# Fetching the first tile's experts beside the last mLSTM cells, with private buffers for its mixer

## The reference

```python
h = modulate(rmsnorm(x, n1), sh1, sc1)
mq, mk, mv, mo, gt, aq, ak, av = split_cols(h @ w_in)
m_out = mlstm_mixer(...)          # both directions, chunk by chunk: a recurrence over C, n, m
a_out = attn_latent(...)          # windowed attention with sinks, 8 heads
x = x + g1 * (concat([m_out, a_out]) @ w_out)
h2 = modulate(rmsnorm(x, n2), sh2, sc2)
q = h2 @ w_q                      # 8 heads x 2 halves of 128
va, ia = top_k(q_a . sub_a, 16); vb, ib = top_k(q_b . sub_b, 16)
top, pos = top_k(va[:, None] + vb[None, :], 16)        # 16 of 256 pairs, per head
eidx = ia * 128 + ib at pos;  gates = softmax(top)
a = gelu(h2 . u_tab[eidx])                              # 128 experts per token
x = x + g2 * sum(gates * a * v_tab[eidx])
```

## Time and profile before

| what | us |
|---|---|
| median of three runs | 3685.37 (3685.03 to 3698.58) |
| span of the profiled execution | 3682.8 |
| PE matmul busy | 2644.4 (72%) |
| DVE busy | 2453.7 (67%) |
| POOL busy | 1459.0 (40%) |
| ACT busy | 990.0 (27%) |
| moved by DMA | 1365.12 MB, 371 GB/s over the span |
| of it the gathers of experts | 1208.03 MB |

### The profile page before, as it was taken

How to read it: one execution, slowest core, us unless ns; L and a number is a source line. 1 busy time by engine, 2 the same in 40 slices (tenths; PEclk the granted TensorE clock), 3 DMA queues, 4 the chain that set the end, 5 groups by cost and what they waited for, 6 DMA issues and landing times.

```text
span 3682.8 us, 31091 instructions
## 1 busy us (share of the span) xinstructions
PE 2644.4 (72%) x9770; PEld 1042.0 (28%) x9770; DVE 2453.7 (67%) x5523; ACT 990.0 (27%) x2700; POOL 1459.0 (40%) x1300
## 2 busy tenths in 40 slices
PE   7999888687877878866566567557656755775655
PEld 3455567333333333312121112112111211221111
DVE  3666435776787678648857677685767768576655
ACT  1223333442433244422122122212212221221111
POOL 0110023443454455434444444444444444444443
PEclk9999889899989989889799789879977987987677
DMA  7222446899999999999999999999999999999999
GB/s 299 95 97 94 163 125 204 333 410 422 416 421 426 425 412 420 389 424 414 427 427 427 427 423 427 422 417 424 416 427 420 427 420 423 424 417 427 411 427 380
DMA packets 224537, 1365.12 MB, mean 371 GB/s; under 512 B 25194, under 2 KB 36074, under 8 KB 75890
## 3 DMA queue, kind: packets, MB, share of 16 engines
q0 software_dynamic: 165888, 1208.03, 78.4%
q1 hardware_dynamic: 50992, 134.74, 10.1%
q10 hardware_dynamic: 7492, 20.36, 1.4%
HBM read 1334.05 MB, written 28.99 MB: 370 GB/s over the span
## 4 chain that ended last, share of the span: by engine, by line
DMA 40%; PE 20%; DVE 15%; issue 4%; POOL 4%; ACT 4%; SPq 0%; ACTq 0%; POOLq 0%; DVEq 0%
DMA fx_ring<-arg_uv,fx_eidx 38%; PE fx_acc L1396 11%; DVE fx_ring L1846 8%; POOL fx_ring L1109 4%; PE at_sP L1241 3%; ACT fx_weighted_pick L1542 2%; PE at_aP L1203 1%; DMA rt_wq<-arg_w_q 1%; DVE rt_rest L1708 1%; DVE rt_ab L1710 1%; DVE rt_rest L1706 1%; DMA rt_w_q<-arg_w_q 1%; PE at_sP L1269 1%; ACT fx_gelu L1538 1%; PE at_sP L1187 1%
## 5 line engine op out<-in xcount | busy, mean ns | idle before, releaser
L1396 PE MATMUL fx_acc<-fx_ring,fx_weighted_pick 128*64 128x512 f32 x4608 | 1417.7, 747 | 929.8 <-ACT fx_weighted_pick L1542 908.3
L1109 POOL DMA_INDIRECT fx_ring<-arg_uv,fx_eidx x1152 | 1317.0, 1143 | 1634.7 <-PE fx_acc L1396 1444.5
L1846 DVE CUSTOM_DVE_ANT_0 fx_ring<-fx_ring,fx_h 128x1024 f32<-128x1024 f32 x1152 | 1411.8, 1237 | 774.0 <-DMA fx_ring<-arg_uv,fx_eidx 769.5
L1396 PEld LDWEIGHTS fx_acc<-fx_ring,fx_weighted_pick 128*64 128x64 f32 x4608 | 327.0, 158 | 1903.7 <-ACT fx_weighted_pick L1542 1368.4
L1538 ACT ACTIVATE fx_gelu<-fx_dot 128x2 f32<-128x2 f32 x576 | 117.1, 203 | 2116.2 <-DVE fx_dot L1846 2115.7
L424 PE MATMUL in_z<-w_in,in_hT 128*128 128x512 f32 (+1 forms) x864 | 352.4, 566 | 7.3 <-PEq L97 7.3
L1542 ACT ACTIVATE fx_weighted_pick<-fx_weighted_pick,fx_gelu 128x64 f32<-128x64 f32 x1152 | 338.0, 340 | 55.1 <-ACT fx_gelu L1538 2.2
L424 PEld LDWEIGHTS in_z<-w_in,in_hT 128*128 128x128 f32 x864 | 163.6, 192 | 177.3 <-issue 172.0
L1269 PE MATMUL rt_qP<-rt_w_q,rt_h2T 128*128 128x512 f32 x384 | 193.6, 629 | 9.4 <-DMA rt_w_q<-arg_w_q 9.4
L384 POOL COPY in_turned<-in_heads 128x320 f32<-128x320 f32 x9 | 9.1, 1010 | 320.1 <-DVE in_heads L579 320.1
L1241 PE MATMUL at_sP<-at_w_out,at_mixT 128*128 128x512 f32 x288 | 133.3, 606 | 0.9 <-DVE at_mixT L1601 0.9
(11 more groups left out here) (300 smaller groups left out, 2450.4 us busy)
## 6 DMA issues: line engine op xcount, KB each, us to landing
rt_wq<-arg_w_q SPq DMA_DIRECT2D x44, 512.0 KB, 7.8
fx_ring<-arg_uv,fx_eidx POOLq DMA_INDIRECT x1152, 12.7
in_ada_w<-arg_w_ada SPq DMA_DIRECT2D x32, 512.0 KB, 4.0
ml_qkT<-qkT_scratch SPq DMA_DIRECT2D x18, 512.0 KB, 4.2
ada_w<-arg_w_ada SPq DMA_DIRECT2D x8, 1024.0 KB, 13.8
w_in<-arg_w_in SPq DMA_DIRECT2D x16, 512.0 KB, 16.4
rt_w_q<-arg_w_q SPq DMA_DIRECT2D x16, 512.0 KB, 32.7
kv_scratch<-in_kv ACTq DMA_DIRECT2D x9, 768.0 KB, 3.3
```

The source lines that it names most:

```text
L1109: pool.indirect_dma_start(out=ring[j][:], out_offset=None, in_=io.uv, in_offset=bass.IndirectOffsetOnAxis(ap=eidx[t % 2][:, i:i + 1], axis=0),
L1396: mm = pe.matmul(acc[b][cg * TOKS:(cg + 1) * TOKS, :], wsel[:, i % (2 * FILL), :], ring[i % GROUP][:, D + b * 512:D + (b + 1) * 512], star ...
L1846: dve.tensor_tensor_reduce(out=ring[j][:, 0:D], in0=ring[j][:, 0:D], in1=h2r[t % 2][cg][:], scale=1.0, scalar=0.0, op0=ALU.mult, op1=ALU.a ...
```

## The change

Three things are changed together.

1. *Order.* In the first 34 routing steps of tile 0 only every third brings a cell step. `begin` follows, now without a wait for the cells: it waits only until the mixer of tile 0 has stored its result. Three more cell steps stand between `begin` and pair 0, and then two cell steps to a pair in pairs 0 to 12 (`CELL_PAIRS` = 13). The mixer of tile 1 starts at pair 13.
2. *Pace.* At tile 0 the routing of tile 0 ends at pair 16 as before, nothing is routed in pairs 17 to 29, and the routing of tile 1 takes one step to a pair from pair 30 to pair 63. Mixer steps stand beside every pair of tile 0 from 13 on; beside pairs 0 to 24, every odd one to 50, and 51 to 63 at tile 1.
3. *Memory and banks.* The cells' buffers must live on while tile 0's experts are fetched. So tile 0's mixer gets buffers of its own (`first`), the other mixers a second set (`later`) in a room that the cells' buffers and later `w_q` share. The ring moves behind that room. `w_out` and its gate are loaded twice, once into each set, and DVE scales `w_out` by the head norm twice. The cells use the two PSUM banks that belonged to the mixers (`other`), and tile 0's mixer and routing those of the experts' sum.

The core of the diff:

```diff
     def due(t, r):
+        if t == 0:
+            return r >= CELL_PAIRS
         if t == STREAMED - 1:
             return r < WQ_AT
-        return t == 0 and r < SUBS or 17 <= r < 23 or r >= 51 or r % 2
+        return r < 25 or r >= 51 or r % 2

     def pace(t, r):
+        if t == 0:
+            return int(r < 17 or r >= 2 * SUBS)
...
     def cells_beside(k):
         if k < TURN:
             return 1
-        if k < TURN + 11:
-            return int(k % 3 > 0)
-        return 1 + int(k % 4 > 0)
+        return int(k % 3 == 0)
...
-        for _ in cells:
-            pass
         begin()
+        for _ in range(3):
+            next(cells)
...
                 pair(t, r)
...
+                if t == 0 and r < CELL_PAIRS:
+                    for _ in range(2):
+                        next(cells, None)
+                if t == 0 and r == CELL_PAIRS - 1:
+                    for _ in cells:
+                        pass
...
+        later = mixer_buffers(1)
+        with ExitStack() as room:
+            w_q = room.enter_context(nc.sbuf_tensor("rt_w_q", [P, KD, 2 * D], F32))
+        held = sb("mixer_room", [P, ROOM])
+        first = mixer_buffers(0)
...
+                def load_weights(cnd):
+                    m = later if cnd else first
+                    sp.dma_start(m.gate1[:], g.gate_dram[cnd:cnd + 1, :].to_broadcast([P, D])).then_inc(s_g1, 16)
+                    for k in range(KD):
+                        sp.dma_start(m.w_out[:, k, :], io.w_out[k * P:(k + 1) * P, :]).then_inc(s_wo, 16)
...
+                        if k == 0 and t == 1:
+                            load_head(1)
+                            load_weights(1)
...
                 def begin():
-                    pool.wait_ge(s_hd, UNITS)
-                    for d in range(2):
-                        pool.wait_ge(s_hst[d], 16 * TILES)
+                    pool.wait_ge(s_x1o, 16)
                     for n in range(DEPTH):
                         fetch(n)
```

More of the change, by code:

```diff
@@ L804, in mix_and_experts @@
         gex = sb("rt_gexp", [P, PH, TOPK])
[L806 to L833 removed]
+        wq = wq2 + h2r[0]
         acc = [psum(f"fx_acc{i}") for i in range(2)]
[L836 removed]
+        other = [psum(f"at_sP{i}") for i in range(2)]
         aP = psum("at_aP")
@@ L839, in mix_and_experts @@
         cP = psum("rt_cP", (P, 4, P))
-        eP = acc[0][:].rearrange("p (h n) -> p h n", n=P)
-        oE = acc[0][:].rearrange("p (h n) -> p h n", n=256)
-        R = [x[:].rearrange("p (h n) -> p h n", n=256) for x in (acc[1], qP[0], qP[1])]
+        eP = other[0][:].rearrange("p (h n) -> p h n", n=P)
+        oE = other[0][:].rearrange("p (h n) -> p h n", n=256)
+        R = [x[:].rearrange("p (h n) -> p h n", n=256) for x in (other[1], qP[0], qP[1])]
         misc = cP[:].rearrange("p h n -> p (h n)")
-        qP0, cP0 = ST, aP[:].rearrange("p (h n) -> p h n", n=P)
+        first.ST, later.ST = acc, other
+        qP0, cP0 = acc, aP[:].rearrange("p (h n) -> p h n", n=P)
         s_in = sem("ml_state_cleared")
@@ L947, in load_head @@
                             sp.wait_ge(s_nm, t * AH)
-                        sp.dma_start(mask[:], io.att_mask[t]).then_inc(s_mk, 16)
+                        sp.dma_start(m.mask[:], io.att_mask[t]).then_inc(s_mk, 16)
                 def load_h(t):
+                    m = first if t == 0 else later
                     if t < 2:
@@ L1068, in _ @@
                 load_head(0)
-                sp.dma_start(x1[:], io.x[0]).then_inc(s_x, 16)
-                sp.dma_start(gate1[:], g.gate_dram[0:0 + 1, :].to_broadcast([P, D])).then_inc(s_g1, 16)
-                for k in range(KD):
-                    sp.dma_start(w_out[:, k, :], io.w_out[k * P:(k + 1) * P, :]).then_inc(s_wo, 16)
+                sp.dma_start(first.x1[:], io.x[0]).then_inc(s_x, 16)
+                load_weights(0)
                 for m in range(2 * WQ):
@@ L1434, in route @@
                     for k in range(steps_of(t)):
-                        x1t = x1r if t else x1[:]
+                        x1t = x1r if t else first.x1[:]
                         if k == TURN - 3:
```

201 lines of the change are left out of this document (103 added, 98 removed).

## The result

The changed kernel takes **3770.8 us** (median of 4 runs, 3764.6 to 3775.8) against 3690.0 for the kernel before on the same chip (4 runs, 3685.0 to 3698.6): **1.0222** times, 95% interval 1.020 to 1.0245. The forecast was 3699 with a range up to 3725. The sign was right, the size was not: 81 us in place of 13, outside the range. The profiled execution has a span of 3765.4 us against 3682.8.

What follows compares the result with a forecast made beforehand. From the first expert fetch on, the kernel was taken as a DMA byte stream at 420 GB/s. Terms -51.6 + 35 + 12 + 10 + 8 = +13.4 on span 3682.8 gave 3696.2, predicted 3699 with run offset; range 3675 to 3725.

Steps and rivals of the forecast that it cites:

- Start of the fetch: Before the first expert fetch on POOL: it starts at 612.5 us instead of 664.09, 51.6 us earlier; both ends 603 and 630.
- Bytes behind the start: After the first fetch: cell loads and stores, w_out and its gate again, 14.7 MB at 420 GB/s, +35 us.
- DMA idle among the cells: First pairs of tile 0, with cell steps beside them: 9.0 us per pair against 6.9 of DMA, +12 us.
- Tile 0 to tile 1: Between pair 63 and tile 1's first gather: the ring drains awaiting tile 1's experts, 8 to 13 us idle, +10 taken.
- PE in pairs 30 to 63: Tile 0, tile 1's routing beside a mixer step in every pair: PE lacks slack, between 0 and 20 us, +8 taken.
- so nothing: Mixers ending at pair 17 of tile 2 instead of pair 29: bytes move, none saved, DMA's share already full, no cost.
- tiles 3 to 8 must keep their 323 us each: Sign to check in the last six tiles: their time stays 323 us each, 1939/6, as before the change.
- Cells hidden under the stream: Rival 1, pairs with cells: engines overlap better, period falls toward 6.9 us, idle 12 vanish, 3677 us; chance 0.17.
- PE as the bound: Rival 2: period 10.5 us at a lowered clock (+16), 20 us lost from pair 30 on (+12), 3727; chance 0.17.
- A late fetch: Rival 3, start of the fetch: query weights set the pace, first fetch at 630 instead of 612.5, 3716 us; chance 0.08.
- Table switches at twice the price: Rival 4, ACT among the cells: another 1.28 us at each of fifteen table switches, +19, 3718 us; chance 0.06.
- rivals 2 to 4: The slower cases: PE becomes the bound (0.17), fetch hardly starts earlier (0.08), table switches hold ACT twice as long (0.06).

## Why the prediction was wrong

Three steps failed: the address of the ring had no term, the changed `due` of tile 1 was put at nothing, and the idle time among the cells was two and a half times the forecast's. In order:

**Start of the fetch: right.** 611.92 against 612.5, released by the gates of the routing and by no store of a cell.

**Bytes behind the start: right.** Up to fetch 24 DMA moved 65.2 MB against 51.9 before, 13.3 more, where the forecast had 14.7. With all cells ahead, 24 pairs took 138.8 us; with the tables alone 128.1. The 10.7 are the second w_out and gate (11 forecast). At the end some 5 are left, 38.5 for the buffers less 34 for the address; the errors of these medians don't tell 5 from 11.

**DMA idle among the cells: mechanism right, size off.** "+12 us, and 11 more or less for each us of the period." The idle time was some 30 us. The period was 10.1, not 9.0, which is 12 us more by the forecast's own rate. In the piece of the loop shown, 705.53 to 715.70, the links are those forecast, with the filling of weights (1.05) in it and a start of 0.3 on POOL. What the forecast's 9.0 left out is the lowered clock. Of the eight pairs' matmuls from 671 to 744 us five took 3.3 to 3.7 us instead of 1.94, such as these:

```profile
690.83 3.68 PE L1426 MATMUL fx_acc<-fx_ring,fx_weighted_pick 128*64 128x512 f32 x8 [1.47 <-ACT fx_weighted_pick L1573]
...
732.95 3.31 PE L1426 MATMUL fx_acc<-fx_ring,fx_weighted_pick 128*64 128x512 f32 x8 [3.48 <-ACT fx_weighted_pick L1573]
```

Since they stand in the loop, that is 7.5 us over eight pairs, 0.9 a pair by estimate: nearly the whole miss. The forecast named it ("so 9.0 may become 10.5") and left it out of the sum. The rest lies in the first eight pairs, where cell loads stood behind gathers: POOL waited 9.8 us for the values of a cell, and two fetches came 13 us after the one before. At the hand-over to tile 1's mixer TensorE stood 8.9 us for the head's queries and fetch 18 came 15.2 us after fetch 17, which makes the stretch from fetch 16 to 24 7 us longer than with the cells ahead. That "it costs DMA nothing" nearly held: its share from 756 to 812 us was 0.97, some 2 us idle. Start, the cells' own bytes (24) and idle time together were forecast at -16; taking the cells back out of the changed kernel measured +12.

**Tile 0 to tile 1: right in idle DMA.** "8 to 13 us idle, I take 10." The gap between the fetches of pairs 63 and 64 was 23.7 us where 5.4 is usual, since POOL waited 20.8 us for the gates: three pairs and the side steps between them come first, because TensorE and VectorE did every pair and mixer step before the closing one. But the gathers already issued kept the DMA engines at work for most of it. Their share, in the column before the last, was 1.01 or more up to 1050 us and then

```profile
1050.00:1055.00 5.00, 3.28 (x14) 1.47 (x16) 4.93 (x7) 3.65 (x8) 0.00 (x0) 0.82 0.74 304
1055.00:1060.00 5.00, 5.00 (x28) 3.05 (x24) 4.78 (x15) 1.77 (x4) 0.00 (x0) 0.84 0.20 52
1060.00:1065.00 5.00, 3.33 (x18) 1.34 (x16) 1.50 (x5) 3.10 (x6) 3.25 (x4) 1.00 0.59 200
```

which is 7.5 us idle, at the lower end of the forecast. The 18 us that the fetches lose there hold in addition 4.1 MB more than before (31.1 against 27.0 from fetch 60 to 72), 10 us.

**PE in pairs 30 to 63: wrong, and it was in the next tile.** The forecast had 8 us there; fetches 24 to 60 took 2.6 us less than before, with DMA full (1.02) although PE was 94% busy. The 21 us came in tile 1, from the changed `due`, which the forecast did not price at all beyond "so nothing": mixer loads among query weights that have two buffers. About 11 of the 21, with the end of the pause among them, are idle DMA.

**What had no step: the address of the ring.** 34 us, the largest single error. The sentence that failed is the test written for it, "tiles 3 to 8 must keep their 323 us each": they took 328, 1967/6. The change moved buffers, and the forecast read the move for lifetimes and bytes only, never for where in a partition they begin.

By medians of the runs the causes are 34 (address), 33 (tables), 5 (second w_out) and 12 (cells beside pairs): 84 for 81 measured. These are differences along one chain of kernels, from the one before to the changed one, so their sum had to come near 81 and proves nothing; each carries an error of several us.

**The rivals.** Cells hidden under the stream: no, the period would have had to be under 7.8, and even 9.0 gains nothing. PE as the bound: half, its period came (10.1 for 10.5), and from the lowered clock that it named, but its 20 us from pair 30 on did not. A late fetch: no. Table switches at twice the price: no; in the changed kernel a gelu stands right behind a load,

```profile
699.99 1.28 ACT L1569 ACT_TABLE_LOAD   x1
...
701.29 0.20 ACT L1569 ACTIVATE fx_gelu<-fx_dot 128x2 f32<-128x2 f32 x1
```

0.02 us after its end. The chances of rivals 2 to 4 add up to 0.31, where the forecast wrote 0.28, which makes its chance of "slower" 0.43 instead of 0.40.

What stays open: which part of the first eight pairs' loss is the landing of cell loads and which the lowered clock (0.77 there), what the second w_out costs between 5 and 11 us, and why the tables of tile 0 alone leave DMA idle behind fetch 104. No run takes these apart.

## What to carry to other kernels

When a change moves buffers, look at where each DMA destination begins before anything else: here a ring of 8 KB rows off a 256-byte grid cost about 1% of the whole kernel at an unchanged DMA share, and one unused 32-byte buffer showed it. Look for a pause in the DMA share as well as in the gap between two fetches: here 18 us lost between fetches held 7.5 us of idle DMA. A step table is a plan for a queue as much as for engines: steps that load through two buffers were late here when they met other loads on the same queue, and when they came two at a time. And work moved beside a stream is not hidden by being short: its links add to the loop between one pair and the next, by the order that each engine keeps.

## Not expected of the hardware

Thirty-two unused bytes ahead of a gather's destination made the kernel 1.17% slower (1.0117) with no instruction changed, and 256 or 512 bytes did nothing (0.9998 and 1.0003). Of the offsets tried, 32 cost more in tiles 3 to 8 (35.6 us) than 128 (24.8) or 160 and 192 (28).
